# Joining the last gate to the output projection, and reordering the first layer's input and modulation

## What is computed

```python
def layer(x, xc):            # latent and context tokens
    sh1, sc1, g1, sh2, sc2, g2 = split(silu(c) @ ada_w[layer] + ada_b[layer], 6)
    h  = x * (1 + sc1) + sh1           # the same for the context, from c_ctx
    z  = concat(h, hc) @ w_in[layer]   # its columns feed the four groups
    ...
    # the DeltaNet group's output, per head of 64 channels, gate z_:
    o  = rms_norm(o, norm_g) * silu(z_)
    ...
    y  = concat([ya, yb, yr, yd])
    x  = layer_norm(ALPHA * x + g1 * (y @ w_out[layer]), ln1_g, ln1_b)
    x  = layer_norm(ALPHA * x + g2 * squared_relu_mlp(...), ln2_g, ln2_b)
```

## Time and profile before

| | us |
|---|---|
| median of 3 runs | 4320.06 (4316.73 to 4320.37) |
| the profiled execution | 4329.14 |
| its span, first to last instruction | 4327.3 |
| PE busy | 3989.3 (92%) |
| DVE busy | 2041.8 (47%) |
| ACT busy | 1131.9 (26%) |
| POOL busy | 937.3 (22%) |
| DMA, mean over the span | 42 GB/s |

### The profile page before, as it was taken

One profiled execution on the slowest core, in us unless ns is written; L12 is line 12 of the kernel. 1 busy time (PEld: TensorE's weight loads), 2 busy tenths in 40 slices (PEclk: granted clock), 3 DMA queues, 4 the chain that ended last, 5 costly groups with the idle time before them and its releaser, 6 DMA issues. The chain is left out here.

```text
span 4327.3 us, 77639 instructions
## 1 busy us (share of the span) xinstructions
PE 3989.3 (92%) x33178; PEld 3278.3 (76%) x33178; DVE 2041.8 (47%) x3705; ACT 1131.9 (26%) x2456; POOL 937.3 (22%) x671
## 2 busy tenths in 40 slices
PE   6999988989979999999998999889899799999997
PEld 5655987778867888888886557778688677888886
DVE  3344546544456433333356344566344555443346
ACT  3344224233323111111115443232333311110012
POOL 0000110032202433333321000100223114444441
PEclk8898999999989999999998998999899899999999
DMA  4311000100010111111111110000100011111111
GB/s 168 117 79 59 21 30 1 76 3 3 3 49 10 39 39 39 39 39 39 39 38 69 59 79 30 20 21 20 48 3 3 21 39 39 49 48 48 48 49 49
DMA packets 27552, 181.00 MB, mean 42 GB/s; under 512 B 2560, under 2 KB 6912, under 8 KB 12032
## 3 DMA queue, kind: packets, MB, share of 16 engines
q1 hardware_dynamic: 25968, 173.69, 10.8%
q10 hardware_dynamic: 1296, 3.10, 0.2%
HBM read 168.39 MB, written 8.39 MB: 41 GB/s over the span
## 5 line engine op out<-in xcount | busy, mean ns | idle before, releaser
L1298 PE MATMUL ps<-Yn_parts,ring_parts 128*128 128x512 f32 (+1 forms) x3888 | 803.2, 368 | 11.5 <-issue 7.7
L1298 PEld LDWEIGHTS ps<-Yn_parts,ring_parts 128*128 128x128 f32 x3888 | 674.4, 190 | 137.3 <-issue 9.9
L1298 PE MATMUL ps<-temp_parts,ring_parts 128*128 128x512 f32 (+1 forms) x2560 | 727.9, 370 | 3.9 <-DVE Hn_parts L2437 3.9
L2731 POOL TENSOR_TENSOR ring_parts<-ring,consts 128x2048 fp32r<-128x2048 f32 x64 | 295.6, 4619 | 1209.1 <-DMA ring<-in_ff 1093.6
L741 PE MATMUL ps<-ring_parts,Xn_parts 128*128 128x256 f32 x2560 | 514.6, 296 | 28.3 <-DVE ring_parts L1986 12.8
L2384 DVE SCALAR_TENSOR_TENSOR Xn<-ps,mods,Xn 128x256 f32<-128x256 f32 (+1 forms) x364 | 251.8, 692 | 604.0 <-PE ps L1298 503.3
L1298 PEld LDWEIGHTS ps<-temp_parts,ring_parts 128*128 128x128 f32 x2560 | 466.4, 190 | 88.3 <-DVE Hn_parts L2437 5.9
L1298 PE MATMUL ps<-Hn_parts,ring_parts 128*128 128x512 f32 (+1 forms) x1280 | 472.1, 369 | 0.0
L741 PEld LDWEIGHTS ps<-ring_parts,Xn_parts 128*128 128x128 f32 x2560 | 425.8, 199 | 32.3 <-issue 23.5
L1825 ACT ACTIVATE Yn<-ps 128x256 f32<-128x256 f32 (+1 forms) x160 | 88.7, 554 | 1265.7 <-PE ps L1298 1265.7
L2491 DVE TENSOR_TENSOR Yn<-Yn 128x256 f32<-128x256 f32 (+1 forms) x160 | 200.6, 1254 | 406.2 <-ACT Yn_parts L1827 406.2
(11 more groups left out here) (310 smaller groups left out, 5956.0 us busy)
## 6 DMA issues: line engine op xcount, KB each, us to landing
ring<-in_ff SPq DMA_DIRECT2D x64, 1024.0 KB, 4.7
ring<-in_ada SPq DMA_DIRECT2D x22, 2048.0 KB, 8.9
ring<-in_halves SPq DMA_DIRECT2D x28, 1024.0 KB, 4.8
Xn<-in_x SPq DMA_DIRECT2D x2, 5120.0 KB, 25.0
Hn<-in_ada SPq DMA_DIRECT2D x2, 2048.0 KB, 20.9
kept_x<-Xn SPq DMA_DIRECT2D x4, 1024.0 KB, 4.0
Xn<-kept_x SPq DMA_DIRECT2D x1, 4096.0 KB, 14.9
Hn<-in_halves SPq DMA_DIRECT2D x2, 1024.0 KB, 7.6
```

What stands on the lines that cost most here:

```text
L1298: m = pe.matmul(ps[:, bank, 0:hi - lo], w[a][:, k, j * P:(j + 1) * P], x[b][:, k, lo:hi], start=(k == 0 and part == 0), stop=(k == k_n - 1 ...
L2731: link(TT(by(half_hi[s]), by(half[s]), spread(ones, 1, HALF // P), ALU.mult))
```

## The change

In three parts.

**Gate joined to the projection.** The barrier between them is gone on all four engines. ACT squares the DeltaNet output in two halves and DVE sums each half when it comes. The multiplication by the norm's gain leaves DVE: the gain is now one value per partition (channel), given as the scale of ACT's copies from PSUM to Y. DVE's first `split_low` moves behind the last gated pair. ACT makes the first segment's two high blocks (channels 4 to 7 first, then 0 to 3) ahead of its last two PSUM copies, when all gated rows are written and the first three copies done. PE's very first product of the projection is a `first_product`: the same 24 matmuls, first the 16 with H_hi (waiting for each half of it), then the 8 with Y_lo.

**Input by segments.** SP loads the context's segment of X where the whole X was, and segments 1 and 2 behind the two half chunks, each with its own semaphore (`x_part_1`, `x_part_2`, names that before were `x_saved_...`).

**Start.** The two `ada_rows` of the first calls use banks 7 and 6, without a wait between them. ACT splits the weight half before the modulation, DVE directly behind the context's; DVE then modulates segments 1 and 2 before the low parts of 1; items 0 and 1 come ahead of segment 2's high parts on ACT and ahead of its low parts on DVE.

The core of the diff:

```diff
-                        sp.dma_start(X[:, :, :], d["x"]).then_inc(sems["x_in"], 16)
+                        sp.dma_start(X[:, :, 0:NCTX], d["x"][:, :, 0:NCTX]).then_inc(sems["x_in"], 16)
+                if L == 0:
+                    for c, (lo, hi) in enumerate(SEGMENTS):
+                        if c:
+                            sp.dma_start(X[:, :, lo:hi], d["x"][:, :, lo:hi]).then_inc(sems[f"x_part_{c}"], 16)
...
+            def first_product(w, lo, hi):
+
+                halves_ = (range(4, KT), range(4))
+                for n_, ks in enumerate(halves_):
+                    pe.wait_ge(sems["h_high"], nth("h_high", n_ + 1))
+                    for k in ks:
+                        for a in range(2):
+                            pe.matmul(ps[:, 0, 0:hi - lo], w[a][:, k, 0:P], H_hi[:, k, lo:hi], start=(k == 4 and a == 0), stop=False)
+                pe.wait_ge(sems["h_split"], nth("h_split", 1))
+                for ks in halves_:
+                    for k in ks:
+                        m = pe.matmul(ps[:, 0, 0:hi - lo], w[0][:, k, 0:P], Y_lo[:, k, lo:hi], start=False, stop=(k == 3))
+                m.then_inc(sems["prod"], tally("prod"))
...
-                    m = pe.matmul(ps[g:g + 32, 7, :], silu_c[:, 2 * k:2 * k + 32], w[:, k, :],
+                    m = pe.matmul(ps[g:g + 32, 7 - slot_, :], silu_c[:, 2 * k:2 * k + 32], w[:, k, :],
...
             def ada():
                 ada_rows(0)
-                ada_kept()
                 ada_rows(1)
...
+                    if n_ == 0:
+                        first_product(halves_[i], *cols[c])
+                        continue
...
                 gate_turn(gate_dn)
-                ln.barrier()
                 project_out(L)
...
-            def modulate(L, shift, scale):
-
-                for c in range(len(SEGMENTS)):
-                    modulate_high(L, c)
-                    if c == 0:
-                        split_high()
-
-            def mla_prep():
-
-                for i in range(2 * NT + 3):
+            def mla_prep(L):
+
+                split_high()
+                modulate_high(L, 0)
+                modulate_high(L, 1)
+                mla_item(0)
+                mla_item(1)
+                modulate_high(L, 2)
+                for i in range(2, 2 * NT + 3):
...
-                A(g_["sq"].rearrange("p a b -> p (a b)"), g_["o"], ACT.Square).then_inc(sems["sq_done"], tally("sq_done"))
+            def gate(g_, L):
+
+                lo, hi = tokens(L)[0]
+                sq = flat(g_["sq"])
+                for c in range(2):
+                    n_ = NT * 128
+                    A(sq[:, c * n_:(c + 1) * n_], g_["o"][:, c * n_:(c + 1) * n_], ACT.Square).then_inc(sems["sq_done"], tally("sq_done"))
                 A(flat(g_["th"]), flat(g_["z"]), ACT.Tanh, scale=0.5).then_inc(sems["g_tanh"], tally("g_tanh"))
-                if g_ is gate_dn:
-                    split_high()
+                split_high()
                 act.wait_ge(sems["g_veps"], nth("g_veps", 1))
                 A(g_["root"], g_["root"], ACT.Sqrt).then_inc(sems["g_rstd"], tally("g_rstd"))
-                if g_ is gate_dn:
-                    split_high()
+                split_high()
                 for c in range(NT // 2):
+                    if c == 3:
+                        act.wait_ge(sems["g_y"], nth("g_y", NT // 2))
+                        for n_ in range(3):
+                            act.wait_ge(sems["yT_sb"], nth("yT_sb", n_ + 1))
+                        for k in (4, 0):
+                            A(H_hi[:, k:k + 4, lo:hi], Y[:, k:k + 4, lo:hi], ACT.Copy).then_inc(sems["h_high"], tally("h_high"))
                     act.wait_ge(sems["yT_mm"], nth("yT_mm", c + 1))
-                    A(Y[:, g_["rows"]:g_["rows"] + 2, 2 * c * P:2 * (c + 1) * P], ps[:, 5 + c % 2, :].rearrange("p (a b) -> p a b", a=2), ACT.Copy)\
-                        .then_inc(sems["yT_sb"], tally("yT_sb"))
+                    A(Y[:, g_["rows"]:g_["rows"] + 2, 2 * c * P:2 * (c + 1) * P], ps[:, 5 + c % 2, :].rearrange("p (a b) -> p a b", a=2), ACT.Copy,
+                      scale=g_["gain"]).then_inc(sems["yT_sb"], tally("yT_sb"))
...
+                act.wait_ge(sems["yT_sb"], nth("yT_sb", NT // 2))
                 act.sem_inc(sems["out_free"], 1)
                 for c, (lo, hi) in enumerate(cols):
                     for k in (0, 4):
-                        A(H_hi[:, k:k + 4, lo:hi], Y[:, k:k + 4, lo:hi], ACT.Copy).then_inc(sems["h_high"], tally("h_high"))
+                        if c:
+                            A(H_hi[:, k:k + 4, lo:hi], Y[:, k:k + 4, lo:hi], ACT.Copy).then_inc(sems["h_high"], tally("h_high"))
...
+                modulate_full(L, 0)
+                split_low()
+                modulate_low(0)
+                modulate_full(L, 1)
+                modulate_full(L, 2)
+                modulate_low(1)
+                mla_item(0)
+                mla_item(1)
+                modulate_low(2)
+                for i in range(2, 2 * NT + 2):
...
-                dve.wait_ge(sems["sq_done"], nth("sq_done", 1))
-                link(dve.tensor_reduce(g_["root"], g_["sq"], AX.X, ALU.add))
+                for c in range(2):
+                    n_ = NT * H // 2
+                    dve.wait_ge(sems["sq_done"], nth("sq_done", c + 1))
+                    m = dve.tensor_reduce(g_["root"][:, c * n_:(c + 1) * n_], g_["sq"][:, c * n_:(c + 1) * n_, :], AX.X, ALU.add)
+                link(m)
                 TS(g_["root"], g_["root"], 1.0 / 64, EPS, ALU.mult, ALU.add).then_inc(sems["g_veps"], tally("g_veps"))
                 dve.wait_ge(sems["g_tanh"], nth("g_tanh", 1))
-                link(STT(th, th, 1.0, flat(g_["z"]), ALU.add, ALU.mult))
-                th_ = heads(th, NT * 256 // n_gain)
-                link(TT(th_, th_, spread(g_["gain"], 1, NT * 256 // n_gain), ALU.mult))
-                if g_ is gate_dn:
-                    split_low()
+                STT(th, th, 1.0, flat(g_["z"]), ALU.add, ALU.mult)
                 dve.wait_ge(sems["g_rstd"], nth("g_rstd", 1))
                 link(dve.reciprocal(g_["rs"], g_["root"]))
...
                     m.then_inc(sems["g_y"], tally("g_y"))
+                split_low()
```

48 lines of the change are left out of this document (18 added, 30 removed).

## The result

| | median, us | lowest to highest | runs |
|---|---|---|---|
| kernel before | 4320.82 | 4316.73 to 4329.01 | 6 |
| changed kernel | 4293.11 | 4275.99 to 4297.97 | 6 |

The ratio is 0.9925, with a 95% interval of 0.9903 to 0.9946: 32.4 us faster, somewhere between 23 and 42. The changed kernel was measured once more beside the first group of experiments: 4290.55 us against 4315.90, ratio 0.9948 (0.9932 to 0.9963), 22.4 us. The forecast was 4296.2 in a range of 4288 to 4306. The profiled execution took 4297.97 us; its span is 31.1 us shorter than that of before, where the sum said 23.9.

What follows compares the result with a forecast made beforehand. TensorE was taken to set the end nearly everywhere, waiting in the serial bridge between DeltaNet scan and projection. 8.5 + 10.8 + 4.6 = 23.9 us off the median 4320.06 gave 4296.2, range 4288 to 4306.

Steps and rivals of the forecast that it cites:

- Bridge, layer 0: Between DeltaNet scan and projection in layer 0: PE's first product starts at 1227.1 instead of 1235.65, 8.5 us earlier.
- Bridge, layer 1: Same bridge in layer 1: PE can start at 3439.7 instead of 3450.49, a gain of 10.8 us.
- The rival of a clock that rises sooner: At the projections' start: transposes count towards a clock rise, saving up to 5.4 us more, 4290.8; chance 12%.
- The join does less than it says: In the bridges: ACT's blocks or scale operand run slower, PE stops behind first products, half of 19.3 lost, 4306; chance 9%.
- Holds by under 1 us: Layer 0's projection: DVE's low part for the second segment ready at 1234.3, wanted by PE at 1235.
- The input's segments come late: Program start: by the bound of pieces segments land late, 0 to 9.6 us of difference, 4301 to 4306; chance 15%.
- The full queue: Input DMA at 0.429 MB per us: segment 1 lands at 40.0, segment 2 at 44.9, before wanted, costing nothing.
- the rival's price: Input DMA in pieces: 3.1 us more per MB, from 8.0 against 4.9 us, segment 2 landing at 60.5.
- The start: Modulation and first tiles: PE's third tile starts at 60.5 instead of 65.11, 4.6 us earlier.
- The 1 us of loss that I allowed: First stage: segment 2's high parts on ACT make the third tile's square 1.7 late; 1 us of loss allowed.
- what its start gains should reach the end: Behind the bridge PE hardly waits, so its earlier start should reach the end unless something behind it comes late.
- The slower rival: In both projections PE gets no full clock, each us of matmul work costs one more, 4361.8; chance 2%.

Runs made afterwards that it cites:

- the first group of experiments: On one chip beside the kernel before: gate and projection edits alone, start edits alone, changed kernel with input in one DMA, and changed kernel repeated (4290.55 us).
- warm: Changed kernel plus 14 unused matmuls ahead of the gate's transposes in each layer; 4293.16 us, ratio 0.9941 to the kernel before.
- low_before: Changed kernel with VectorE's low part of the output weights put back ahead of the reciprocal; 4293.32 us, ratio 0.9943 to the kernel before.
- start_only: Kernel before with only the start's edits (two PSUM banks, weights split first, input by segments, new order); 4319.75 us, ratio 1.0011.
- the delayed starts: Six memsets on VectorE ahead of the context's modulation, in the kernel before (4340.49 us, ratio 1.0033) and in the changed kernel (4313.29 us, ratio 0.9970).
- before_again: The kernel before, unchanged, measured once more against itself; 4327.66 us, ratio 0.9997.
- no_first: Changed kernel without the first product's high matmuls taken ahead of VectorE's low parts; 4306.72 us, ratio 0.9968 to the kernel before.
- late_before: Kernel before with six memsets on VectorE ahead of the context's modulation, delaying the start; 4340.49 us, ratio 1.0033.
- start_again: Kernel before with only the start's edits, measured a second time; 4326.40 us, ratio 0.9994.

## Why the prediction was right

**Bridge, layer 0: 8.5 us predicted.** The product's start moved by 8.5 (26.5 to 18.0), and each landmark lies where the working has it: the reciprocal directly behind the root, 8.3 us after the square (8.1 predicted), the last wait that for the low part of the weights. At layer 1 **10.1** arrive. Of the other 1.6 us the shorter cold stretch explains half: 3.9 us at the low level instead of 5.4 saves 0.8, since the clock is 1.2 GHz there instead of 2.4. The rest arises later in unchanged code and is not explained.

**Bridge, layer 1: 10.8 us predicted.** The product's start moved by 10.9, **12.3** arrive at the end. Here the cold stretch is 3.1 us instead of 5.9, which saves 1.4, all of the difference.

**The rival of a clock that rises sooner** was right in its direction: I gave up to 5.4 us to it and 12%; about 3.1 came beyond the forecast (22.4 less 19.3), of which the cold stretches explain 2.2 by the figures above. Its mechanism, transposes that count towards a rise, was argued and not tested: the shorter gap and the shorter cold stretch come together, and no run separates them. warm, with TensorE busy through most of the gap, held the clock in layer 0 and lost it right behind the product's start in layer 1. What sets it stays open. This is the term that was mis-sized in the forecast: I left the cold stretch at its old length.

**The join does less than it says** didn't come: no wait inside the first three products. "Holds by under 1 us" for the second segment's low parts was true, and narrower than it sounds: they were ready at 1237.43 and taken up at 1237.48. In low_before and in warm, where this balance shifts by about a microsecond or two, the wait is there, 1.09 and 2.13 us.

**The input's segments come late** didn't come. The full queue was the right bound: 1738 packets at 0.415 MB per us against 0.429 for 141, 3% less for pieces of 1 and 2 KB. Segment 1 was there at 45.33 and segment 2 at 49.22, when DVE took them up. Segment 2 landed at 47.0, 2.1 us later than the forecast 44.9. At 0.415 MB per us that fits the 0.65 MB of weights that ACT loads from 37.2 and 37.6 on, which the sum left out. The Trainium skill, "DMA: Bandwidth & Descriptors", Specifications, had 512 B as the least size at line rate; this run agrees with it for a full queue. The prediction read the rival's price wrongly. The 8.0 us of the earlier trace rows were not measured on an empty queue: this half was issued 0.37 us behind the one that took 4.9, in the kernel before:

```profile
1265.88 0.33 SPq L670 DMA_DIRECT2D ring<-in_halves  x1
1266.25 0.99 SPq L659 DMA_DIRECT2D Hn<-in_halves  x1
```

It landed 3.5 us behind the first. The same pair issued at 1209.1, both in one piece per partition, landed 2.5 us apart (4.7 and 6.7 us). So the rows of 1 KB cost about 1 us per MB there, not 3.1, and no run has a transfer in pieces alone on the queue.

**The start, 4.6 us predicted.** Third tile 5.9 us sooner. The first tile came at 45.6 (46.2 predicted). The barrier fell at 37.2, not 38.1, since the adaLN rows of both products now run in one piece of 5.83 us, where they took 8.0 with their pause of 0.71. The 1 us of loss that I allowed, without putting it into the sum, did come, as the wait of 1.10 us at 69.45; 5.2 us are left at the stage's end. The kernel's time shows of them between nothing (1.0011 and 0.9994 alone) and 6.3 (at equal clock). Here the step "what its start gains should reach the end" is not confirmed: start_only's interval leaves at most 0.4 us, and only the delayed starts and the comparison at equal clock speak for it.

**The slower rival**, a clock that stays low in the projection, is excluded: 1.00 from 1234.0 on.

**The account.** In landmarks the change is worth 22.4 + 5.2 = 27.6 us, against 23.9 predicted; medians within one group give 27.7 and 25.4, the ratios 32.4 and 22.4. That the forecast time came so near is in part luck: the bridges gave 3.1 us more than their share of the sum, and the start's 4.6 don't show by themselves. The 31.1 us between the two profiled runs are, in order of time: the start -5.9, from there to layer 0's bridge +8.7 (1144.06 to 1152.71 us, unchanged code but for the wait of 1.10), the bridge and MLP -9.9, layer 1 up to its bridge -10.4 (1124.4 to 1114.0, unchanged code), the rest -13.6. The +8.7 and the -10.4 are of the size by which executions differ anyway: over the 14 traces the first of these stretches takes 1136.6 to 1152.8 us, and before_again has 1114.3 for the second.

## What to carry to other kernels

Between two stages of a PE-bound kernel, list what the first matmul really reads, and order the helpers' queues by that: here the work of one product (24 matmuls) could be split so that its two-thirds that need no low parts cover the making of the low parts, worth 2.4 and 4.5 us by itself. The start of the product behind a serial bridge could be costed here to within 0.1 us from the durations of one trace; what the clock adds behind it was not. Judge terms of this size by landmarks in traces of several variants, not by the kernel's time, and before crediting a stage with a gain run the old kernel again: unchanged code differed by 11 and by 16 us.

## What the runs showed of the hardware that I had not expected

- The same program gives two lengths for one stage: layer 1's latent attention took near 240.7 us in before, start_only and no_first, near 229.4 in before_again, late_before and all others but start_again, which had 227, with the same instructions.
- The mean granted clock orders the runs of one kernel: from 0.954 to 0.959 some 3 to 5.5 us for each 0.001 in the kernel before, and hardly anything below that (4329.1, 4329.6, 4327.9 us at 0.952, 0.953, 0.954).
- A queue that is full lost only 3% with 1738 packets in 11 us in place of 141.
- A product that started 2.4 us later (no_first) put the next layer 3.3 us later, one that started 4.5 us later the end 5.4; 0.4 and 1.3 of that is a longer stretch at 1.2 GHz behind it.
- With fourteen dummy matmuls ahead of the transposes the clock stood at 1.00 when the product started, in both layers; it stayed there in layer 0 and fell for about 3.4 us in layer 1 (0.70 over 5.6 us), with the same code.
